# ScalarE issues the store of score rows and the rounding of weights ahead of the store of the gates

## The chip, the cores and the metric

The kernel runs on one core of one Trainium2 chip. The metric is the device time of one execution in microseconds (us). A run of the kernel is one such time; medians of several runs are compared.

## What is computed

The reference is a model in float32 over 512 tokens of width 1024: two layers with a gated feed-forward, a mixer of pooling and windowed attention and a second feed-forward each, then a block with a gated delta rule and an mLSTM, and last a layer of experts chosen by product keys. The change lies in that last layer, which cut to its core is:

```python
qry = (t @ w_q).reshape(n_tok, 8, 2, 128)
scores = einsum("thpd,hpkd->thpk", qry, sub_keys)          # 128 keys for each half
s_top, i_top = top_k(scores, 16)
cand = s_top[:, :, 0, :, None] + s_top[:, :, 1, None, :]
cand_idx = i_top[:, :, 0, :, None] * 128 + i_top[:, :, 1, None, :]
best, pos = top_k(cand, 16)
idx = take_along_axis(cand_idx, pos)                        # 8 x 16 experts of 16384 for each token
gate = softmax(best)
act = gelu(einsum("td,thkd->thk", t, u_tab[idx]))
out = einsum("thk,thkd->td", gate * act, v_tab[idx])
```

## The kernel before

It doesn't gather experts. It multiplies all tokens with all 16384 rows of the tables and weighs each score with a dense matrix of gates, which is zero for experts that a token hasn't chosen. Every product of 32-bit numbers is made as three matmuls of rounded parts (helper `product`, L925 to L927): high by high, low by high, high by low.

**Weights** come as tiles of 128 x 2048 numbers in one fixed order through two slots. SP loads `raw` (L373); ScalarE rounds it to `w_hi` (`split_hi`, L427), after the tile has landed and the slot has been used up; GpSimd makes `w_lo = raw - w_hi` in four pieces (L390) and counts `lo_written`; TensorE waits for that count, and SP loads the next tile into the slot after it. So rounding of tile n + 2 is issued by ScalarE after tile n has been used.

**Score tiles run ahead.** 36 tiles of the first table (`AHEAD_TILES`) are multiplied before the gates are ready. Each makes two score rows (e = 0, 1; eight products of three matmuls each), which ScalarE passes through Gelu into `stage` (`stage_row`, L740). `store_tile` then waits for that activation, stores `stage` to `s_store` in DRAM (L745, 512 KB) and rounds the weights two tiles on.

**Gate building** is the stretch of the change (3117 to 3378 us of the trace). The 512 tokens go in 8 chunks of 64, and a chunk in 16 quads of four tokens. VectorE writes one-hot rows for a quad into one of four `hot` buffers: four TENSOR_SCALARs (L2410) and one TENSOR_TENSOR (L2413), once the quad four back has been multiplied. TensorE multiplies them, four matmuls of 128 x 128 for a quad (L1631), into one of four banks, once that bank has been evicted. ScalarE evicts a bank into `g_buf` (L785), which has two buffers of one chunk each; a chunk waits for the store of the chunk two back. TensorE's order is written out: four quads, half of a score row, and so on, so that one chunk has 16 quads and both rows of one score tile. After eight quads and each score row ScalarE runs `stage_row`. At the end of a chunk it issues the chunk's gates to `g_store` in DRAM (L791, 4 MB, in runs of 1 KB) and then calls `store_tile`. Both are DMAs on ScalarE's own queue.

**Behind the chunks** four more score tiles follow without quads. After the second of them ScalarE waits for all gates' stores and loads the first group (L806, L809), VectorE weighs the scores with the gates, and the second table's products begin.

Names and lines that matter: L427 rounding, L390 low part, L740 Gelu of a score row, L745 score store, L785 eviction of gates, L791 gates' store, L1631 one-hot products, L925 to L927 score products, L2410 and L2413 one-hot rows, L806 load of gates.

Of the kernel before, what the change touches and what calls it, by code (L numbers as in the profile page):

```python
# [29 lines left out]
TT = TOKENS // P  # L30
# [35 lines left out]
CHOICE_TILES = 6  # L66
# [49 lines left out]
def build(nc, x_in, weights, gains, small, pool_w, consts, rope, second, level_masks,  # L116
# [3 lines left out]
    with stack:  # L120
# [15 lines left out]
        def sem(name):  # L136
            if name not in sems:
                sems[name] = stack.enter_context(nc.semaphore(name))
            return sems[name]
# [263 lines left out]
        def _(act):  # L403
# [15 lines left out]
            def split_hi(tile, i=None, per=2):  # L419

                if i is None and tile >= TILES:
                    return
                slot, half = tile % 2, tile // 2
                act.wait_ge(tile_landed[slot], 16 * (half + 1) if i is None else i * (8 * per) + 16 * (half + 1))
                if tile >= 2:
                    act.wait_ge(tile_used, tile - 1 if i is None else i * per + (tile - 1))
                act.activation(w_hi[:, slot, :], raw[:, slot, :], ACT.Copy).then_inc(hi_written, 1)  # L427
# [257 lines left out]
            def experts():  # L685
# [44 lines left out]
                def stage_row(n, e, i=None):  # L730

                    if e == 0:
                        act.wait_ge(sem("s_ahead_done"), n + 1 if i is None else i * 2 + (n + 1))
                        if n >= 2:

                            there = 16 * (n // 2)
                            act.wait_ge(s_stored[n % 2], there if i is None else i * 16 + there)
                    else:
                        act.wait_ge(tile_used, TABLE_AT + n + 1 if i is None else i * 2 + (TABLE_AT + n + 1))
                    c_st.up(act.activation(stage[:, n % 2, e, :], banks[e][:, :], ACT.Gelu))  # L740

                def store_tile(n, i=None):
                    target = n if i is None else act.snap(i * 2 + n)
                    c_st.held()
                    act.dma_start(s_store[target], stage[:, n % 2]).then_inc(s_stored[n % 2], 16)  # L745
                    split_hi(TABLE_AT + n + 2, i)
# [25 lines left out]
                for c in range(CHUNKS):  # L772
                    for half in range(2):
                        with act.Fori(0, CHUNK // 32) as i:
                            c_ev.loop(i, 4)
                            for b in range(4):
                                q = CHUNK // 4 * c + CHUNK // 8 * half + b
                                at = act.snap(i * 16 + (CHUNK // 2 * half + 4 * b))
                                act.wait_ge(sem("quad_done"), i * 4 + (q + 1))

                                if c >= 2:
                                    act.wait_ge(stored[c % 2], 16 * (c // 2))
                                else:
                                    act.wait_ge(sem("keys_landed"), 32)
                                c_ev.up(act.activation(  # L785
                                    g_buf[:, c % 2, :, bass.ds(at, 4)],
                                    banks[quad_banks[b]][:, :].rearrange("p (t i) -> p i t", t=4), ACT.Copy))
                        c_ev.end(CHUNK // 32)
                        stage_row(CHOICE_TILES * TT + c, half)
                    c_ev.held()  # L790
                    act.dma_start(g_store[:, c].rearrange("g j n -> j g n"),  # L791
                                  g_buf[:, c % 2].rearrange("p (g e) t -> p g (e t)", g=GROUPS)).then_inc(stored[c % 2], 16)
                    store_tile(CHOICE_TILES * TT + c)


                landed = [sem("gates_landed0"), sem("gates_landed1")]
# [100 lines left out]
            for layer in range(LAYERS):  # L897
                ffn(2 * layer)
                mix(layer)
                ffn(2 * layer + 1)  # L900
            second_mixer()
            experts()

        @block.tensor
# [1740 lines left out]
```

## Time and profile before

| | |
|---|---|
| median of 3 runs | 4459.71 us |
| lowest, highest | 4449.06, 4461.06 us |
| profiled execution | 4452.29 us, span 4450.5 us |
| mean granted TensorE clock, as a share of full | 0.974 |
| TensorE matmul busy | 4218.7 us, 95% of the span |
| VectorE, ScalarE, GpSimd busy | 1950.5, 1313.2, 1795.3 us |
| gates' stores (L791) | 8 of 4 MB, 13.6 us from issue to landing |
| score stores (L745) | 36 of 512 KB, 3.2 us |

The profile is of one execution, so steps in it are compared with its own time and not with the median. The busy shares are means over the whole kernel; the stretch of the gate building is 261 us of it and is read by itself, in its own waits and timelines. A DMA's row on an engine's queue (ACTq, SPq) is the time that its issue holds the queue, not the transfer.

### The profile page before, as it was taken

What the parts mean: (1) busy time and instruction counts of PE and PEld (TensorE: products, weight loads), DVE (VectorE), ACT (ScalarE), POOL (GpSimd) and SP (SyncE); (2) the same over time, 40 slices, a digit from 0 to 9 for tenths busy, and PEclk for the clock granted to TensorE, in tenths of its full rate; (3) what the DMA queues carried; (4) which work ended last, traced back from release to release, by engine and by line L of the source; (5) the groups of instructions that cost most, each with busy time, mean ns of one, the idle gap of its engine ahead of it and who ended that gap; (6) DMA issues with size and microseconds to landing.
All of it is one profiled execution on the core that took longest, in us unless ns stands there. A gap on an engine that the chain in (4) does not pass through costs nothing.

```text
span 4450.5 us, 54686 instructions
## 1 busy us (share of the span) xinstructions
PE 4218.7 (95%) x20004; PEld 3501.2 (79%) x20004; DVE 1950.5 (44%) x3700; ACT 1313.2 (30%) x1599; POOL 1795.3 (40%) x1328
## 2 busy tenths in 40 slices
PE   8999899999999999999987889999888999999998
PEld 6888668888888777887866878787787888888887
DVE  2213443212212443211387763695884666333333
ACT  3222243223222143222231123333333222222322
POOL 4444234444444334444320014445113555554553
PEclk9999999999999999999998999999999999999999
DMA  3222112222222112223110002333456555333332
GB/s 123 95 104 88 64 69 95 94 96 93 95 103 97 67 67 85 94 96 108 57 48 1 1 20 105 109 128 133 154 177 217 193 194 195 126 113 132 113 123 76
DMA packets 127504, 461.30 MB, mean 104 GB/s; under 512 B 8080, under 2 KB 73872, under 8 KB 84752
## 3 DMA queue, kind: packets, MB, share of 16 engines
q1 hardware_dynamic: 48960, 351.29, 22.1%
q10 hardware_dynamic: 78416, 108.22, 7.0%
q8 instruction: 90, 1.47, 0.1%
q14 instruction: 38, 0.31, 0.0%
HBM read 404.96 MB, written 54.53 MB: 103 GB/s over the span
## 4 chain that ended last, share of the span: by engine, by line
issue 51%; POOL 25%; PE 23%; DVE 0%; POOLq 0%; ACT 0%; ACTq 0%; DVEq 0%
POOL w_lo L390 25%; PE bank L925 8%; PE bank L926 8%; PE bank L927 8%; POOLq L394 0%; DVE x L2511 0%; POOLq L397 0%; DVE weighed L2441 0%; DVE w_mix_lo L2448 0%; DVE sq_last L1759 0%; PE bank L967 0%; PE bank L960 0%; ACT stage L740 0%; POOLq L390 0%; DVE sq_last L1760 0%
## 5 line engine op out<-in xcount | busy, mean ns | idle before, releaser
L390 POOL TENSOR_TENSOR w_lo<-raw,w_hi 128x512 fp32r<-128x512 f32 x1324 | 1795.1, 1387 | 2621.7 <-ACT w_hi L427 2621.6
L925 PE MATMUL bank<-h_hi,w_hi 128*128 128x512 f32 x3232 | 1283.6, 397 | 53.6 <-POOL w_lo L390 26.9
L926 PE MATMUL bank<-h_lo,w_hi 128*128 128x512 f32 x3232 | 1267.6, 392 | 0.0
L927 PE MATMUL bank<-h_hi,w_lo 128*128 128x512 f32 x3232 | 1267.5, 392 | 0.0
L427 ACT ACTIVATE w_hi<-raw 128x2048 fp32r<-128x2048 f32 x331 | 632.4, 1911 | 1207.9 <-PE bank L927 1129.8
L925 PEld LDWEIGHTS bank<-h_hi,w_hi 128*128 128x128 f32 x3232 | 613.7, 190 | 189.2 <-issue 50.1
L927 PEld LDWEIGHTS bank<-h_hi,w_lo 128*128 128x128 f32 x3232 | 612.4, 189 | 130.6
L926 PEld LDWEIGHTS bank<-h_lo,w_hi 128*128 128x128 f32 x3232 | 614.0, 190 | 127.4 <-issue 1.8
L925 PE MATMUL bank<-w_mix_hi,w_hi 128*128 128x512 f32 x1024 | 398.4, 389 | 0.9 <-ACT stage L740 0.9
L927 PE MATMUL bank<-w_mix_hi,w_lo 128*128 128x512 f32 x1024 | 398.3, 389 | 0.0
L926 PE MATMUL bank<-w_mix_lo,w_hi 128*128 128x512 f32 x1024 | 398.3, 389 | 0.0
L2460 DVE TENSOR_TENSOR x<-x,bank 128x512 f32<-128x512 f32 x256 | 172.6, 684 | 299.8 <-PE bank L927 298.2
L925 PE MATMUL bank<-act_hi,w_hi 128*128 (+1 forms) x704 | 273.9, 389 | 0.0
L926 PE MATMUL bank<-act_lo,w_hi 128*128 (+1 forms) x704 | 273.9, 389 | 0.0
L927 PE MATMUL bank<-act_hi,w_lo 128*128 (+1 forms) x704 | 273.9, 389 | 0.0
L1774 DVE SCALAR_TENSOR_TENSOR x<-bank,x 128x512 f32<-128x512 f32 x56 | 38.1, 681 | 453.5 <-PE bank L927 453.5
L1802 DVE TENSOR_TENSOR up_s<-bank,rstd 128x512 f32<-128x512 f32 x88 | 60.9, 692 | 383.1 <-PE bank L927 382.9
L925 PEld LDWEIGHTS bank<-w_mix_hi,w_hi 128*128 128x128 f32 x1024 | 192.2, 188 | 41.4 <-issue 1.3
L927 PEld LDWEIGHTS bank<-w_mix_hi,w_lo 128*128 128x128 f32 x1024 | 192.2, 188 | 39.8
L926 PEld LDWEIGHTS bank<-w_mix_lo,w_hi 128*128 128x128 f32 x1024 | 192.2, 188 | 39.8
L456 ACT ACTIVATE act_hi<-up_s 128x512 f32 (+1 forms) x88 | 55.6, 631 | 461.2 <-DVE up_s L1804 461.2
L1631 PE MATMUL bank<-hot 128*128 128x128 f32 x1024 | 139.2, 300 | 39.1 <-ACT g_buf L785 32.7
(372 smaller groups left out, 4442.8 us busy)
## 6 DMA issues: line engine op xcount, KB each, us to landing
raw<-weights SPq DMA_DIRECT2D x331, 1024.0 KB, 4.8
g_store<-g_buf ACTq DMA_DIRECT2D x8, 4096.0 KB, 13.6
g_in<-g_store ACTq DMA_DIRECT2D x32, 1024.0 KB, 5.5
s_store<-stage ACTq DMA_DIRECT2D x36, 512.0 KB, 3.2
s_in<-s_store ACTq DMA_DIRECT2D x18, 1024.0 KB, 7.5
x<-x_in SPq DMA_DIRECT2D x1, 2048.0 KB, 10.4
out<-x SPq DMA_DIRECT2D x8, 256.0 KB, 2.2
keys_sb<-keys ACTq DMA_DIRECT2D x1, 1024.0 KB, 4.7
```

The lines of the kernel that those rows point to most:

```text
L390: ins = pool.tensor_tensor(w_lo[:, slot, cols], raw[:, slot, cols], w_hi[:, slot, cols].bitcast(F32), ALU.subtract)
L427: act.activation(w_hi[:, slot, :], raw[:, slot, :], ACT.Copy).then_inc(hi_written, 1)
L456: c_act_hi.up(act.activation(act_hi[:, at, :], prod[:, :], ACT.Copy))
L925: pe.matmul(out_ap, w_hi[:, slot, cols], m_hi, start=start, stop=False)
L926: pe.matmul(out_ap, w_hi[:, slot, cols], m_lo, start=False, stop=False)
L927: return pe.matmul(out_ap, w_lo[:, slot, cols], m_hi, start=False, stop=stop)
L1631: ins = pe.matmul(banks[quad_banks[q % 4]][:, n * P:n * P + P], hot[:, q % 4, n, 1, :], hot[:, q % 4, n, 0, :], start=True, stop=True)
L1774: c_x.up(dve.scalar_tensor_tensor(x[:, n, :], banks[n][:, :], scale, x[:, n, :], ALU.mult, ALU.add))
L1802: c_us.step(dve.tensor_tensor(up_s[:, :], banks[up_bank][:, :], rstd[:, :], ALU.mult))
L2460: c_x.up(dve.tensor_tensor(x[:, d, :], x[:, d, :], banks[4 + d % 4][:, :], ALU.add))
```

## The change

At the end of each chunk `store_tile` moves ahead of the wait for the evictions and the gates' store. `store_tile` holds the wait for the Gelu, the score store (L745) and the rounding of the next weights (L427). What is transferred, waited for and counted stays the same.

```diff
                         c_ev.end(CHUNK // 32)
                         stage_row(CHOICE_TILES * TT + c, half)
+                    store_tile(CHOICE_TILES * TT + c)
                     c_ev.held()
                     act.dma_start(g_store[:, c].rearrange("g j n -> j g n"),
                                   g_buf[:, c % 2].rearrange("p (g e) t -> p g (e t)", g=GROUPS)).then_inc(stored[c % 2], 16)
-                    store_tile(CHOICE_TILES * TT + c)
```

## Rows read from the trace of the kernel before

**Rows 1.** The page's head.

```profile
span 4450.5 us, 54686 instructions
```

**Rows 2.** Waits, 3117 to 3400 us: who waited <- for whom: total us, times, longest.

```profile
ACT w_hi L427 <- issue: 64.1, 8, 8.9
...
DVE hot L2410 <- PE bank L1631: 33.2, 7, 5.3
...
PE bank L1631 <- ACT g_buf L785: 32.7, 7, 4.9
...
PE bank L925 <- POOL w_lo L390: 5.6, 1, 5.6
```

**Rows 3.** Timeline of ACT around a chunk's end: start us, us, what [idle before].

```profile
3115.69 0.34 ACTq L745 DMA_DIRECT2D s_store<-stage  x1
3116.13 1.91 ACT L427 ACTIVATE w_hi<-raw 128x2048 fp32r<-128x2048 f32 x1 [0.47 <-ACT stage L740]
...
3150.92 0.60 ACT L740 ACTIVATE stage<-bank 128x512 f32<-128x512 f32 x1 [2.04 <-PE bank L927]
3150.93 0.40 ACTq L791 DMA_DIRECT2D g_store<-g_buf  x1
3151.55 7.55 ACTq L745 DMA_DIRECT2D s_store<-stage  x1
3159.21 1.91 ACT L427 ACTIVATE w_hi<-raw 128x2048 fp32r<-128x2048 f32 x1 [7.68 <-issue]
3161.02 2.04 ACT L785 ACTIVATE g_buf<-bank 128x512 f32 x4
```

**Rows 4.** The same at the end of the last chunk.

```profile
3378.14 0.60 ACT L740 ACTIVATE stage<-bank 128x512 f32<-128x512 f32 x1 [2.04 <-PE bank L927]
```

**Rows 5.** Line 745's issues, 3150 to 3379 us: duration ns min/median/max.

```profile
L745 ACTq DMA_DIRECT2D s_store<-stage x8: 7546/7808/8747, 3151.6 to 3378.8; - x8
```

**Rows 6.** Timeline of ACT, a gate load issued just behind a score store.

```profile
3419.48 0.36 ACTq L745 DMA_DIRECT2D s_store<-stage  x1
...
3419.97 1.15 ACTq L806 DMA_DIRECT2D g_in<-g_store  x1
```

**Rows 7.** Timeline of PE, one-hot products and a score row.

```profile
3131.81 3.73 PE L1631 MATMUL bank<-hot 128*128 128x128 f32 x32
...
3138.11 3.73 PE L1631 MATMUL bank<-hot 128*128 128x128 f32 x32
...
3161.75 6.36 PE L1631 MATMUL bank<-hot 128*128 128x128 f32 x32 [4.55 <-ACT g_buf L785]
...
3394.60 0.79 PE L925 MATMUL bank<-h_hi,w_hi 128*128 128x512 f32 x1 [5.62 <-POOL w_lo L390]
```

**Rows 8.** Timeline of DVE; the first two pieces lie under a POOL run.

```profile
3117.69 3.02 DVE L2410 TENSOR_SCALAR hot<-numbers,chosen 128x128 f32<-128x128 f32 x4
...
3124.90 1.10 DVE L2410 TENSOR_SCALAR hot<-numbers,chosen 128x128 f32<-128x128 f32 x4
...
3197.00 2.71 DVE L2410 TENSOR_SCALAR hot<-numbers,chosen 128x128 f32<-128x128 f32 x4 [5.24 <-PE bank L1631]
3199.63 0.68 DVE L2413 TENSOR_TENSOR hot<-numbers,chosen 128x512 f32<-128x512 f32 x1
...
3224.03 0.70 DVE L2413 TENSOR_TENSOR hot<-numbers,chosen 128x512 f32<-128x512 f32 x1
```

**Rows 9.** Timeline of POOL.

```profile
3118.12 5.40 POOL L390 TENSOR_TENSOR w_lo<-raw,w_hi 128x512 fp32r<-128x512 f32 x4 [5.84 <-ACT w_hi L427]
```

**Rows 10.** Busy time of stretches: us, PE, PEld, DVE, ACT, POOL, PEclk, DMA share, GB/s.

```profile
3119.00:3120.00 1.00, 0.00 (x0) 0.00 (x0) 1.00 (x2) 0.60 (x1) 1.00 (x2) 0.65 0.00 0
...
3129.00:3130.00 1.00, 1.00 (x5) 0.78 (x4) 1.00 (x3) 0.53 (x1) 0.00 (x0) 0.73 0.00 0
...
3394.60:3399.51 4.91, 4.91 (x12) 3.90 (x13) 0.00 (x0) 0.00 (x0) 4.88 (x4) 0.53 0.61 214
3399.51:3430.00 30.49, 30.18 (x133) 24.61 (x132) 8.46 (x8) 9.10 (x12) 11.42 (x8) 1.00 0.72 245
```

## The prediction, made before the changed kernel ran

> **What bounds the kernel now.** The profile was read from the page inward: its head (the span is 4450.5 us [rows 1]), then the waits of the one stretch in which the moved lines run, 3117 to 3400 us, then the timelines of ScalarE, TensorE, VectorE and GpSimd there. The reader is to see four waits in the list [rows 2]. ScalarE idles 64.1 us in 8 pieces before the rounding of weights (L427), with no engine named as the releaser ("issue"). TensorE's one-hot products (L1631) wait 32.7 us in 7 pieces for ScalarE's evictions (L785). VectorE's one-hot rows (L2410) wait 33.2 us in 7 pieces for those products. And the score row (L925) waits once, 5.6 us, for GpSimd's low parts (L390). They are one chain, and the ScalarE timeline shows its head [rows 3]: at the end of a chunk the gates' store (L791) is issued at 3150.93 in 0.40 us, the score store (L745) behind it starts at 3151.55 and takes 7.55 us, and only then come the rounding (3159.21) and the next evictions (3161.02). An undisturbed score store takes 0.34 us, with the rounding 0.44 us after its start (3115.69, 3116.13 in the same rows). All 8 behind a gates' store take 7.55 to 8.75 us [rows 4]. So ScalarE's queue is held by the second of two stores, not by the first.
>
> The stretch beats by chunk: the last score row's activation ends a chunk's work, at 3150.92 [rows 3] for the first and 3378.14 [rows 5] for the eighth, (3378.14 - 3150.92) / 7 = 32.46 us each. TensorE could do it in less: a part (four quads and half a score row) takes 3138.11 - 3131.81 = 6.30 us [rows 6], four parts 25.2 us. The rest is the wait of 4.55 us before 3161.75 and the lower clock behind it: the same 32 products take 6.36 us instead of 3.73 us [rows 6], 2.63 us more. 25.2 + 4.55 + 2.63 = 32.4 us: the sum closes, so TensorE with this stall sets the beat today, and VectorE idles under it.
>
> **The change part by part.** Nothing is removed or added: two DMA issues and one rounding swap places in each of 8 chunks. In the new order, from 3150.92: score store at 3151.55 for 0.34 us, rounding at 3151.99, evictions 1.81 us later (3161.02 - 3159.21 [rows 3]) at 3153.80, the first done at 3154.40. TensorE wants that bank at 3161.75 - 4.55 = 3157.20 [rows 6], so its wait goes, with 2.8 us to spare.
>
> The gates' store, now last, is issued at about 3152.1 while the rounding runs. Its own issue, with nothing big ahead of it, is 0.40 us [rows 3]; a load of gates issued 0.49 us behind a score store took 1.15 us [rows 7]. Both ends lie under the rounding (until 3153.90), so it costs nothing; without that cover it would be 0.4 to 1.15 us a chunk. What is held behind it? ScalarE's next DMA is the next chunk's score store, some 29 us later, against a hold of at most 8.75 us. SP's queue comes next: GpSimd finishes the low part about 7 us earlier and SP then issues the next weights into the remaining descriptors. SP's hold has no row; it is between nothing and 8.75 us, and I take it whole: the slot it fills is next rounded two chunks on (the other slot is already full), so nothing waits. The store of gates lands about 1 us later; its buffer is written again two chunks on.
>
> **What is late next: VectorE.** It makes a quad's one-hot rows every (3224.03 - 3199.63) / 15 = 1.627 us [rows 8], 26.0 us per chunk of 16, which is already more than TensorE's 25.2. And it pays for GpSimd. Under the run of low parts at 3118.12, 5.40 us long [rows 9], two quads took 3124.90 - 3117.69 = 7.21 us [rows 8] instead of 3.25: 3.96 us lost. Today most of that run falls into VectorE's idle time: behind the stall four TENSOR_SCALARs take 2.71 us instead of 1.10 [rows 8], 1.6 us lost. In the new order the low parts start at about 3154, when VectorE is working, so the full loss falls due. I take 3.96 us (that run lies wholly in VectorE's work, as the new ones will) and keep 1.6 us and 5.40 us as ends. New beat: 26.0 + 3.96 = 30.0 us, a gain of 2.46 us in each of 7 chunks, 17.2 us. Of the 7.2 us that TensorE gets back, VectorE keeps 4.7.
>
> By the Trainium skill (SBUF - State Buffer, Who interferes with whom) VectorE and GpSimd share a port pair as an exclusive lock, held for a whole instruction, and the other "fully blocks". If that meant the whole run of 5.40 us, the beat would be 31.4 us and this term 7.1 us instead of 17.2. The trace has VectorE getting through between GpSimd's four pieces, with 3.96 of 5.40 us lost.
>
> **The tail.** Behind the eighth chunk TensorE needs the tile whose rounding is held by the 8.75 us store. It waits 5.62 us for the low part before 3394.60 [rows 6] and then runs 12 products in 4.91 us at a granted clock of 0.53 [rows 10]; at the later rate, 30.18 / 133 = 0.227 us each at 1.00 [rows 10], they are 2.72 us. In the new order the low part is ready some 8 us behind the chunk's end, and TensorE wants it after a whole tile, 48 x 0.227 = 10.9 us: the wait goes. Gain 5.62 + 2.19 = 7.8 us. The store of the next score tile comes 11.5 us behind the chunk's end, the gates' store is through its hold at about 10 us; if it were held, the tile it delays is wanted 10 us later still. What follows (loads of gates and scores, weighing) hangs on the score tiles of TensorE and moves forward with them.
>
> **Sum.** 17.2 + 7.8 = 25.0 us. The profiled execution took 4452.3 us (span 4450.5 and 1.8 around it): 4427.3 us by its own time. The median of the runs shown is 4459.7 and their spread 4449.1 to 4461.1; the mean of all four is 4455.5, 3.2 above the profile. I add these 3.2 us: **4431 us**, 0.65% under the median.
>
> **The rivals.** (a) VectorE's loss stays small, since it has a few quads in hand when GpSimd starts: beat 26.0 + 1.6 = 27.6 us, gain 7 x 4.8 + 7.8 = 41.6, 4414 us. For it: four buffers. Against it: where VectorE sets the beat, nothing is in hand. (b) The full block above: 7.1 + 7.8 = 14.9, 4441 us. Against it: 3.96 measured. (c) The change doesn't do what it says: the hold belongs to ScalarE's queue behind a gates' store, whatever comes next, and not to the next DMA. No row shows a compute instruction straight behind L791, so it is open. Evictions would then start at 3152.5 + 7.8 = 3160.3 instead of 3161.02, 0.7 us x 7 = 5 us, and the tail's 7.8 still comes: 12.8, 4443 us. Against it: L791's record ends after 0.40 us, and the next instruction starts. (d) Slower: the clock. VectorE's stop starves TensorE in bites, and under the first such run the granted clock fell (0.65 at 3119) and came back only at 3129 (0.73) [rows 10]. Each us at the lower of the two clocks (1.2 instead of 2.4 GHz) costs TensorE half a us. 10 us of it give 25.2 + 5 = 30.2 us, level with VectorE; from 2 x (32.46 - 25.2) = 14.5 us per chunk on the change loses in the beat. At 24 us per chunk the beat is 37.2, 7 x 4.7 - 7.8 = 25 us slower, 4481 us. Against it: in that first chunk it came back within about 10 us although VectorE set the pace.
>
> **How the numbers follow.** Forecast 0.60 (own range 4420 to 4438: loss 2.7 to 4.5 us per chunk, and the runs' scatter), (a) 0.15, (b) 0.08, (c) 0.10, (d) 0.04, and 0.03 that a gain is given back later unseen. A measurement of this kernel can tell about 0.3%, 13 us, from no change, so the line lies at 4446. Cases (b) and (c) lie close to it: half of their 0.18 counts as same, with the 0.03: same 0.12, slower 0.04, faster 0.60 + 0.15 + 0.09 = 0.84. The range takes in (a) and the near sides of (b) and (c): 4409 to 4446.
>
> **What would show it.** L745 at about 0.34 us in all chunks; no wait of L1631 for L785; L427 about 1.1 us behind L740's start; VectorE busy without a gap from 3116 to the last quad, its waits for L1631 gone, and four-packs of L2410 under L390 near 2 to 3 us; a beat near 30 us; no wait of L925 for L390 at the tail. Case (c) shows as a gap of 7 us between L427 and the next L785. A beat below 28 or above 31 us, or a tail that keeps its wait, would make the prediction wrong.

## Result and profile after

The changed kernel takes 4433.5 us (median of 4 runs, 4430.7 to 4434.7) against 4458.6 us of the kernel before (4 runs, 4449.1 to 4461.1): a ratio of 0.9945, 95% interval 0.9932 to 0.9958, 25.1 us less. A second series (experiment 5) gave 0.9947 (0.9933 to 0.9961). In the prediction the names [rows 4] and [rows 5] are exchanged, and so are [rows 6] and [rows 7]; from here on each name means the group that bears it.

The timeline of ScalarE at the end of the first chunk of the changed kernel (start us, us, what, idle before) answers to [rows 3]; L792 is the gates' store, one line lower than before:

```profile
3158.90 0.60 ACT L740 ACTIVATE stage<-bank 128x512 f32<-128x512 f32 x1 [2.04 <-PE bank L927]
3159.53 0.34 ACTq L745 DMA_DIRECT2D s_store<-stage  x1
3159.97 1.91 ACT L427 ACTIVATE w_hi<-raw 128x2048 fp32r<-128x2048 f32 x1 [0.47 <-ACT stage L740]
3160.00 0.40 ACTq L792 DMA_DIRECT2D g_store<-g_buf  x1
3161.79 2.04 ACT L785 ACTIVATE g_buf<-bank 128x512 f32 x4
...
3188.19 0.60 ACT L740 ACTIVATE stage<-bank 128x512 f32<-128x512 f32 x1 [2.08 <-PE bank L927]
```

The score store is through in 0.34 us, where it took 7.55 us; the rounding starts 1.07 us behind the Gelu instead of 8.29; and the evictions start 2.9 us behind it, straight behind the rounding, instead of 10.1. All eight score stores of the stretch, 3150 to 3379 us (duration ns min/median/max), against [rows 5]:

```profile
L745 ACTq DMA_DIRECT2D s_store<-stage x8: 343/344/351, 3159.5 to 3369.2; - x8
```

The waits from 3117 to 3400 us (who waited <- for whom: total us, times, longest), against [rows 2]:

```profile
PEld bank L1631 <- DVE hot L2413: 28.6, 19, 3.7
PE bank L1631 <- DVE hot L2413: 24.6, 15, 3.5
```

TensorE no longer waits for ScalarE's evictions, nor its score rows for GpSimd, and VectorE's one-hot rows no longer wait for TensorE. In their place TensorE waits 24.6 us for VectorE. The last chunk's Gelu (3368.59) and the first product of the second table (3412.99) close the two sums:

```profile
3368.59 0.60 ACT L740 ACTIVATE stage<-bank 128x512 f32<-128x512 f32 x1 [2.04 <-PE bank L927]
```
```profile
3412.99 0.47 PE L925 MATMUL bank<-w_mix_hi,w_hi 128*128 128x512 f32 x1 [0.93 <-ACT stage L740]
```

**Beat:** (3368.59 - 3158.90) / 7 = 29.96 us, against 32.46: 7 x 2.50 = 17.5 us. **Tail:** 3412.99 - 3368.59 = 44.40 us. The same product of the kernel before started at 3430.62,

```profile
3430.62 0.47 PE L925 MATMUL bank<-w_mix_hi,w_hi 128*128 128x512 f32 x1 [0.93 <-ACT stage L740]
```

which is 52.48 us behind 3378.14 [rows 4]: 8.1 us gained. Together 25.6 us. From there to the end of the span both take 1019.9 us (4432.9 - 3413.0, 4450.5 - 3430.6), so nothing is given back. The two profiled executions differ by only 17.6 us (4434.7 and 4452.3), since that of the changed kernel came to the stretch 8.0 us later (3158.90 against 3150.92). These 8 us arise ahead of every moved line: VectorE's first one-hot row starts at 3124.00 here and at 3116.06 there. They are scatter as far as the record tells, since the profiled execution of the kernel before is one of its fast ones, 6.3 us under its median; the medians, 25.1 us apart, agree with the stretch.

VectorE under GpSimd's run, in the changed kernel:

```profile
3160.63 1.11 DVE L2410 TENSOR_SCALAR hot<-numbers,chosen 128x128 f32<-128x128 f32 x4
3161.66 0.68 DVE L2413 TENSOR_TENSOR hot<-numbers,chosen 128x512 f32<-128x512 f32 x1
3162.26 5.03 DVE L2410 TENSOR_SCALAR hot<-numbers,chosen 128x128 f32<-128x128 f32 x4
3167.21 0.68 DVE L2413 TENSOR_TENSOR hot<-numbers,chosen 128x512 f32<-128x512 f32 x1
```

Four TENSOR_SCALARs that take 1.11 us take 5.03 us: 3.92 us lost in one place. Two narrower looks into the same stretch show how, one instruction a line:

```profile
3163.46 1.29 POOL L390 TENSOR_TENSOR w_lo<-raw,w_hi 128x512 fp32r<-128x512 f32 x1
...
3164.70 1.27 POOL L390 TENSOR_TENSOR w_lo<-raw,w_hi 128x512 fp32r<-128x512 f32 x1
```
```profile
3163.50 1.33 DVE L2410 TENSOR_SCALAR hot<-numbers,chosen 128x128 f32<-128x128 f32 x1
...
3164.75 1.31 DVE L2410 TENSOR_SCALAR hot<-numbers,chosen 128x128 f32<-128x128 f32 x1
```

VectorE gets one short instruction through for each of GpSimd's pieces. The busy time of stretches of it (us; PE, PEld, DVE, ACT, POOL busy; granted clock; DMA share; GB/s):

```profile
3162.00:3166.00 4.00, 4.00 (x24) 3.39 (x23) 4.00 (x5) 1.83 (x4) 4.00 (x4) 1.00 1.04 347
3166.00:3168.00 2.00, 0.12 (x2) 0.06 (x1) 2.00 (x4) 0.60 (x1) 1.20 (x1) 1.00 1.05 348
3168.00:3172.00 4.00, 4.00 (x21) 3.92 (x22) 4.00 (x14) 0.83 (x2) 0.00 (x0) 0.57 1.01 295
3172.00:3174.00 2.00, 2.00 (x13) 1.73 (x12) 2.00 (x7) 0.96 (x2) 0.00 (x0) 1.00 1.07 331
```

TensorE is idle for nearly all of two us with its clock still at full; then, busy again, it is granted 0.57 of full on average for four us (between its two levels, 1.2 and 2.4 GHz), and full clock again from 3172. That costs it 0.43 x 4 = 1.7 us. The seven chunks as a whole, columns as before:

```profile
3158.90:3368.59 209.69, 191.52 (x1233) 173.42 (x1232) 205.56 (x546) 85.62 (x134) 38.41 (x28) 0.95 0.59 193
```

TensorE is idle for 209.69 - 191.52 = 18.2 us of them, 2.6 a chunk. So its own sum nearly closes too, 25.2 + 2.6 + 1.7 = 29.5 of 29.96 us, and the rows alone don't say which of the two engines sets the beat. The experiments do.

### The profile page after: what moved, and what is told of

The parts are those of the page before. It is cut to its first block, busy times and chain, and to the rows that moved or that the text cites. A ratio compares the mean times of both kernels' runs of the same rounds, so it can differ in the third digit from the quotient of the medians.

```text
span 4432.9 us, 54686 instructions
## 1 busy us (share of the span) xinstructions
PE 4220.6 (95%) x20004; PEld 3501.8 (79%) x20004; DVE 1967.3 (44%) x3700; ACT 1313.5 (30%) x1599; POOL 1799.2 (41%) x1328
## 4 chain that ended last, share of the span: by engine, by line
issue 47%; PE 27%; POOL 24%; DVE 2%; DVEq 0%; POOLq 0%; ACT 0%; ACTq 0%
POOL w_lo L390 24%; PE bank L925 8%; PE bank L927 8%; PE bank L926 8%; PE bank L1631 2%; DVE hot L2410 1%; DVE hot L2413 0%; DVEq L2410 0%; POOLq L394 0%; DVE x L2511 0%; POOLq L397 0%; DVE weighed L2441 0%; DVE w_mix_lo L2448 0%; DVE sq_last L1759 0%; PE bank L967 0%
## 5 line engine op out<-in xcount | busy, mean ns | idle before, releaser
L427 ACT ACTIVATE w_hi<-raw 128x2048 fp32r<-128x2048 f32 x331 | 632.5, 1911 | 1147.5 <-PE bank L927 1129.4
L2410 DVE TENSOR_SCALAR hot<-numbers,chosen 128x128 f32<-128x128 f32 x512 | 167.6, 386 | 0.1
```

The costliest lines, as they stand in the source:

```text
L2410: dve.tensor_scalar(hot[:, q % 4, n, 0, :], numbers[:, :], chosen[:, 0, at], chosen[:, 2, at], ALU.is_equal, ALU.mult)
```

## The experiments

Theory V: in the new order VectorE sets the beat, with 26.0 us of one-hot rows and what it loses under GpSimd's run. Its rivals: TensorE sets it (its own 25.2 us, bites and clock); the hold belongs to whatever follows a gates' store; the gain comes from an early rounding as such. Beats are read as above, from the first and last Gelu of a chunk's end.

**1. Only the rounding is moved.** Edit, against the kernel before:

```diff
                     c_ev.held()
                     act.dma_start(g_store[:, c]...).then_inc(stored[c % 2], 16)
-                    store_tile(CHOICE_TILES * TT + c)
+                    split_hi(TABLE_AT + CHOICE_TILES * TT + c + 2)
+                    c_st.held()
+                    act.dma_start(s_store[CHOICE_TILES * TT + c], stage[:, c % 2]).then_inc(s_stored[c % 2], 16)
```

> Order at a chunk's end: gates' store, rounding of weights, score store (before: gates' store, score store, rounding). Only the rounding leaves the held place; the evictions stay behind the held score store. If the hold falls only on the next DMA of ScalarE's queue, the rounding (L427) starts about 1.1 us behind the Gelu's start, the score store is still held for 7.5 to 8.8 us, and the evictions start about 8.3 us behind the chunk's end instead of 10.1. The tail's 7.8 us are gained whole, since they hang on the rounding alone. Beat: 30.0 us if VectorE sets it (26.0 us of one-hot rows + 4.0 us lost under GpSimd, never idle); 25.2 + 2.8 + 2.6 = 30.6 us if TensorE's remaining wait and the lower clock set it. Total 20 to 26 us under before. If instead the hold falls on whatever follows a gates' store, the rounding is held 7.5 us, the tail keeps its wait and the time is that of before.

Measured: 4434.1 us (ratio 0.9948, 0.9932 to 0.9965), as fast as the full change. ScalarE's timeline, and the waits from 3158 to 3370 us:

```profile
3158.57 0.60 ACT L740 ACTIVATE stage<-bank 128x512 f32<-128x512 f32 x1 [2.04 <-PE bank L929]
3158.58 0.40 ACTq L791 DMA_DIRECT2D g_store<-g_buf  x1
3159.08 1.91 ACT L427 ACTIVATE w_hi<-raw 128x2048 fp32r<-128x2048 f32 x1
3159.20 7.55 ACTq L795 DMA_DIRECT2D s_store<-stage  x1
3167.09 2.06 ACT L785 ACTIVATE g_buf<-bank 128x512 f32 x4 [6.10 <-issue]
```
```profile
ACT g_buf L785 <- issue: 44.1, 7, 6.5
...
PE bank L1633 <- ACT g_buf L785: 22.1, 7, 3.3
...
DVE hot L2412 <- PE bank L1633: 0.8, 3, 0.3
```

The rounding passes the gates' store unheld, so the hold doesn't fall on whatever follows. The score store is still held 7.55 us, and ScalarE's evictions and TensorE still wait in all seven chunks, 22.1 us in sum. Yet the beat is (3369.53 - 3158.57) / 7 = 30.14 us, 0.18 above the full change, and the tail is 44.42 us, as long as there: it hangs on the rounding. VectorE's wait is all but gone (0.8 us), and that decides: the stall of TensorE costs next to nothing as long as VectorE doesn't run out of free buffers. It doesn't, because its own loss now falls into the stall: GpSimd's run lies at 3161.07 to 3166.69, TensorE's wait at 3164.84 to 3167.83. In the kernel before, GpSimd's run (3161.19 to 3166.14) found VectorE idle until 3164.06.

**2. A lighter VectorE in the changed order.** From the fifth quad on, the second kind of one-hot row is written for one token of four; the other three keep old rows, so the gates differ:

```diff
-                    c_hot.up(dve.tensor_tensor(hot[:, q % 4, :, 1, :], numbers[:, None, :].to_broadcast([P, 4, P]),
-                                               chosen[:, 1, four, None].to_broadcast([P, 4, P]), ALU.is_equal))
...
+                        one = bass.ds(dve.snap(i * (4 * QUAD_BUFS) + 4 * q), 1)
+                        c_hot.up(dve.tensor_tensor(hot[:, q % 4, 0:1, 1, :], numbers[:, None, :].to_broadcast([P, 1, P]),
+                                                   chosen[:, 1, one, None].to_broadcast([P, 1, P]), ALU.is_equal))
```

> The changed order, and VectorE writes the second kind of one-hot row for one of four tokens instead of four, from the fifth quad on (the other three keep old rows, so the gates are wrong). That takes some 0.35 us from each quad's 1.63. If VectorE sets the new beat of 29.96 us, it falls: 16 x 1.28 + 4.0 = 24.5 us is less than TensorE's 25.2, so the beat becomes TensorE's, 25.5 to 27 us, and the time some 20 to 30 us under that of the changed kernel. If the beat is TensorE's, by the lower clock behind each bite, it stays at 29 us or more.

Measured: 4407.9 us (0.9892, 0.9876 to 0.9909), 25.6 us under the changed kernel. First and last chunk's end:

```profile
3154.48 0.60 ACT L740 ACTIVATE stage<-bank 128x512 f32<-128x512 f32 x1 [2.05 <-PE bank L927]
```
```profile
3341.74 0.60 ACT L740 ACTIVATE stage<-bank 128x512 f32<-128x512 f32 x1 [2.05 <-PE bank L927]
```

(3341.74 - 3154.48) / 7 = 187.26 / 7 = 26.75 us. Taking work from VectorE takes 3.2 us off the beat, so VectorE set it.

**3. The same lighter VectorE in the order of before.**

> The order of before with the same lighter VectorE (the second kind of one-hot row for one of four tokens, from the fifth quad on). If TensorE's stall behind the held score store sets the beat of before, a lighter VectorE gives nothing: beat 32.0 to 32.5 us, time within 4 us of before, VectorE's waits for L1631 grow by what it saves. If VectorE had a part in it, the beat falls towards 30 us or below.

Measured: 4457.9 us (0.9999, 0.9989 to 1.0008): no change. The waits from 3117 to 3400 us:

```profile
DVE hot L2410 <- PE bank L1631: 79.8, 30, 8.9
...
PE bank L1631 <- ACT g_buf L785: 34.8, 7, 6.5
```

VectorE waits 79.8 us instead of 33.2 [rows 2], about what the lighter rows save, and the beat is (3382.69 - 3154.50) / 7 = 32.60 us. The same edit is worth nothing before the change and 25 us behind it: the bound has moved from the stall to VectorE.

**4. What holds the score store.** Order of before, gates' store cut in two, with the waits for it raised to match:

```diff
-                    act.dma_start(g_store[:, c]...).then_inc(stored[c % 2], 16)
+                    act.dma_start(g_store[0:16, c]...).then_inc(stored[c % 2], 16)
                     store_tile(CHOICE_TILES * TT + c)
+                    act.dma_start(g_store[16:32, c]...).then_inc(stored[c % 2], 16)
```

> The order of before, with the gates' store cut into two of 2 MB (half of the groups each): first half, score store, rounding, second half. It measures what holds the score store. If the queue takes a fixed number of runs and holds the next DMA only until the rest is handed on (4096 runs of 1 KB take 13.6 us, the hold ends at about 8.4 us, so some 1600 runs fit), 2048 runs hold the score store for 1 to 1.6 us. If the hold is a share of the store, it is half, 3.9 us. Either way the evictions start early enough for TensorE (under 6 us), and the time is that of the changed kernel, 20 to 28 us under before.

Measured: 4434.4 us (0.9952, 0.9935 to 0.9968), beat (3361.11 - 3151.21) / 7 = 29.99 us. Score stores (L745) and second halves (L794) of the chunks, duration ns min/median/max:

```profile
L745 ACTq DMA_DIRECT2D s_store<-stage x8: 1154/1840/2460, 3151.8 to 3361.7; - x8
```
```profile
L794 ACTq DMA_DIRECT2D g_store<-g_buf x8: 1155/1171/1715, 3153.1 to 3364.3; - x8
```

Half the store holds the next DMA for 1.84 us (median), not for half of 7.81 us. So the hold isn't a share of the store. It fits a queue that takes a fixed number of outstanding runs and holds the next DMA only for the rest; the median is a little over the 1.6 us at most that I had worked out for some 1600 of them, so by this estimate the number is somewhat smaller. Two sizes of store can't show such a limit, and it stays an estimate. Cutting the store is as good as moving it.

**5. The changed kernel again, beside the next one.**

> The changed kernel once more, beside the next one on the same chip: 25 us under before (0.56%), beat 29.9 to 30.0 us.

Measured: 4434.0 us (5 runs, 4433.4 to 4434.2), ratio 0.9947, beat (3368.06 - 3158.38) / 7 = 29.95 us.

**6. GpSimd out of the stretch.** VectorE makes the 8 low parts of the gate building; GpSimd's loop leaves them out. The core of the edit, in VectorE's program (`trips` is the old loop, for a part of the quads):

```diff
+                def low_part(tile):
+                    dve.wait_ge(hi_written, tile + 1)
+                    dve.wait_ge(lo_written, tile)
+                    for piece in range(PIECES):
+                        cols = slice(piece * PIECE, (piece + 1) * PIECE)
+                        ins = dve.tensor_tensor(w_lo[:, tile % 2, cols], raw[:, tile % 2, cols],
+                                                w_hi[:, tile % 2, cols].bitcast(F32), ALU.subtract)
+                    ins.then_inc(lo_written, 1)
...
+                for c in range(CHUNKS):
+                    trips(at, 4 * c + 2 - at)
+                    at = 4 * c + 2
+                    low_part(DVE_LOW + c)
```

> The changed order, and VectorE itself makes the low parts of the 8 tiles rounded during the gate building, each behind the first eight quads of a chunk; GpSimd makes none there. Four subtractions of 128x512 at about 0.62 us each are 2.5 us, against 4.0 us that VectorE loses today under GpSimd's run. If that loss is what lies between VectorE's 26.0 us and the beat of 29.96, the beat becomes 28.5 us, and the time 10 to 13 us less than that of the changed kernel (the first chunk gains too). If the loss isn't a cost of sharing but the beat is set by TensorE's bites and clock, the beat stays at 30 us, as VectorE is away for 2.5 us in one piece here too.

Measured: 4422.2 us (5 runs, 4421.4 to 4423.6), ratio 0.9922 (0.9908 to 0.9936); on the same chip 11.8 us under the changed kernel, and the two sets of runs don't meet. It is the fastest version that computes everything. VectorE's timeline at one low part, and the busy time from the first chunk's end to the last (columns as above):

```profile
3220.35 1.10 DVE L2418 TENSOR_SCALAR hot<-numbers,chosen 128x128 f32<-128x128 f32 x4
3221.38 0.67 DVE L2421 TENSOR_TENSOR hot<-numbers,chosen 128x512 f32<-128x512 f32 x1
3221.98 2.48 DVE L2438 TENSOR_TENSOR w_lo<-raw,w_hi 128x512 fp32r<-128x512 f32 x4
3224.39 1.10 DVE L2418 TENSOR_SCALAR hot<-numbers,chosen 128x128 f32<-128x128 f32 x4
```
```profile
3156.11:3355.30 199.19, 188.44 (x1233) 165.69 (x1232) 195.20 (x576) 85.53 (x133) 0.00 (x0) 1.00 0.61 203
```

199.19 / 7 = 28.46 us. The low part takes 3224.39 - 3221.98 = 2.41 us of it, which leaves 26.05 for the one-hot rows, against 26.0 forecast. The work costs VectorE less when it does it itself than the 3.9 us that it loses beside GpSimd. TensorE's clock is full throughout.

**7. Both: GpSimd out, and a lighter VectorE.** The edits of experiments 2 and 6 together.

> VectorE makes the low parts in the gate building (as in e4) and writes the second kind of one-hot row for one of four tokens from the fifth quad on (as in e2; the gates are wrong). GpSimd is out of the stretch and VectorE needs 16 x 1.28 + 2.5 = 23 us per chunk, less than TensorE's 25.2. If the 26.75 us of e2 were TensorE's 25.2 plus bites under GpSimd's run, the beat is 25.2 to 25.7 us now, and the time about 4400 us. If something else than VectorE and GpSimd keeps TensorE above 25.2 us (ScalarE's evictions, the weights), it stays near 26.7 us.

Measured: 4395.0 us (0.9852, 0.9836 to 0.9869). Busy time from the first chunk's end to the last:

```profile
3154.32:3330.91 176.59, 176.59 (x1233) 163.13 (x1232) 151.24 (x568) 85.53 (x133) 0.00 (x0) 1.00 0.69 229
```

176.59 / 7 = 25.23 us, TensorE busy in all of it: the 25.2 us of [rows 7] are its floor, and neither ScalarE nor the weights stand in its way. Of the 1.5 us by which experiment 2 lies above it, 1.0 is idle time of TensorE (180.41 us busy of 187.26); what the other 0.5 is, no run shows.

**8. The rounding in the middle of the next chunk.**

```diff
                         stage_row(CHOICE_TILES * TT + c, half)
+                        if half == 0 and c > 0:
+                            split_hi(TABLE_AT + CHOICE_TILES * TT + c + 1)
-                    store_tile(CHOICE_TILES * TT + c)
+                    store_tile(CHOICE_TILES * TT + c, later=c < CHUNKS - 1)
```

`later` makes `store_tile` leave its rounding out.

> The changed order, but the rounding of the first seven chunks is put off to the middle of the next chunk, behind its first score row; score store and gates' store stay where the change has them. GpSimd's run then falls into the second half of a chunk. If the beat is VectorE's 26.0 us plus the loss wherever GpSimd runs, it stays at 29.8 to 30.1 us, and the time within 3 us of the changed kernel. If the gain came from an early rounding, the beat goes back towards 31 us or more.

Measured: 4434.3 us (0.9943, 0.9926 to 0.9960), beat (3369.67 - 3159.74) / 7 = 29.99 us. An early rounding as such isn't the gain: without the stall, VectorE's loss is the same wherever GpSimd runs. A late rounding with the stall left in wasn't run.

## Why the prediction was right

**The hold** falls on the next DMA of ScalarE's queue alone. Rival (c) is out: behind L792 at 3160.00 the evictions start at 3161.79, and in experiment 1 the rounding starts 0.50 us behind a gates' store. The issue of the gates' store takes 0.39 to 0.40 us, the lower of my two bounds, under the rounding as said.

**The beat** was forecast at 30.0 and is 29.96 us. The list shows no wait of VectorE's in the seven chunks, GpSimd's run costs it 3.92 us (I took 3.96), and experiments 2, 3, 6 and 7 show that VectorE with this loss sets the beat. (The records of the seven chunks hold 546 of VectorE's 560 instructions, which is why its busy time there reads 205.56 and not 209.69 us.) Rival (a) is out: VectorE's few quads in hand don't spare it the loss. Rival (b), a block for GpSimd's whole run, would have given 31.4 us. The first run lasts 5.24 us here and costs VectorE 3.92. The trace agrees with the lock of the Trainium skill (SBUF - State Buffer, Who interferes with whom) as one held for a single instruction: under the run a TENSOR_SCALAR of VectorE takes 1.30 to 1.33 us where it took 0.28, and one passes beside each piece of 1.27 to 1.54 us. It isn't a block for the whole run. The prediction had the packs of four at 2 to 3 us; the first takes 5.03, since the run here meets one pack of TENSOR_SCALARs and not two quads evenly, and the loss is the same.

**The tail** was forecast at 7.8 us and gave 8.1. The wait for the low part is gone, and the clock is full behind the eighth chunk:

```profile
3368.59:3379.00 10.41, 10.41 (x47) 8.63 (x46) 0.00 (x0) 3.11 (x3) 5.02 (x4) 1.00 0.89 298
```

**The clock**, rival (d), is down for some 4 us behind the first chunk's end, at a mean of 0.57 (0.58 over four us behind each of the next two), where the rival needed 14.5 us a chunk at the lower level. Over the seven chunks the mean granted clock is 0.95, against 0.92 before. The 1.7 us that it costs TensorE lie inside the time that VectorE needs anyway.

**The sum**, 25.0 us, measured 25.1 by the medians and 25.6 in the stretch. The time, 4431 us, is 2.5 us under the median, and that comes from the base: I took the gain off the mean of the runs before (4455.5), which lies 3.1 us under their median. Two rivals are off by a rounding: by their own terms (a) gains 7 x 4.86 + 7.8 = 41.8 us, not 41.6, and (b) 7 x 1.06 = 7.4 us in the beat, not 7.1. Neither moves a line.

Three steps were wrong without moving the sum. I had the gates' store landing "about 1 us later". The DMA lists from 3150 to 3365 us (KB each, median us from issue to landing) of the changed kernel and then of experiment 8 show why it doesn't:

```profile
g_store<-g_buf ACTq DMA_DIRECT2D x7, 4096.0 KB, 18.6
raw<-weights SPq DMA_DIRECT2D x7, 1024.0 KB, 9.1
```
```profile
g_store<-g_buf ACTq DMA_DIRECT2D x7, 4096.0 KB, 14.6
raw<-weights SPq DMA_DIRECT2D x7, 1024.0 KB, 4.8
```

The earlier low part lets SP's weights go while the gates are still leaving; both slow down, the store from 13.6 us before to 18.6 us, the weights from 4.8 to 9.1. With the rounding in mid-chunk they don't meet. It is harmless where buffers are two chunks deep. The last store is issued at 3369.68 and lands 18.1 us later, at 3387.8, and ScalarE issues the load behind it at 3391.78: 4.0 us were left, where a landing after 13.6 us would have left 8.5. The second step is the weight I gave to TensorE's wait. "Its wait goes" was true, but experiment 1 keeps 3.2 us of it in every chunk and has the whole gain; what had to go was VectorE's idling. The third is SP's hold, which I took whole, up to 8.75 us. In the last chunk of experiment 1 SP issues its weights inside ScalarE's hold:

```profile
3370.16 8.79 ACTq L795 DMA_DIRECT2D s_store<-stage  x1
```
```profile
L373 SPq DMA_DIRECT2D raw<-weights x1: 333/333/333, 3377.2 to 3377.2; - x1
```

ScalarE's queue is held until 3378.95, and SP's issue at 3377.2 takes 0.33 us, as it does in every chunk. SP's queue isn't held there. How it fares nearer to the issue of the gates' store, with more of that store outstanding, stays open.

Open too: whether another GpSimd piece size would cost VectorE less wasn't tried.

## What to carry to other kernels

When a large DMA and a small one leave on the same engine's queue, issue the small one and the work that others wait for first, and the large one last, or cut it: the price fell on the next DMA of that queue (7.55 to 8.75 us), not on the large one's own row (0.40). When a stall goes, add up the next engine's work with what it loses beside its neighbour before counting the stall as gain; here 7.2 us of stall and low clock gave 2.5. And an engine's loss beside another can cost more than doing the other's work itself (3.9 against 2.4 us here).

## What was not expected of the hardware

A store of 4096 runs of 1 KB holds the next DMA of its queue for 7.5 to 8.8 us, one of 2048 runs for 1.2 to 2.5 us: the hold grows far faster than the size. And of a stall of 6.1 to 6.5 us on ScalarE, which starved TensorE for 3.2 us in each chunk, the beat felt 0.18 us, since VectorE was slowed in the same time. VectorE loses time beside GpSimd by the instruction: each of its TENSOR_SCALARs of 0.28 us lasts as long as one piece of GpSimd's, about 1.3 us.
